# Moving the second weight slot of a split-precision decoder layer off the 128-byte grid

## The chip, the cores and the metric

The kernel runs on one core of a Trainium2 chip. Its time is device microseconds (us) of that core for one execution; lower is better. SBUF, the on-chip memory, has 128 partitions, and an address below is a byte offset inside a partition. Every tile of the kernel is placed by hand at such an offset.

## The reference

One decoder layer on 512 tokens of width 1024, in float32: a half SwiGLU feed-forward (1024 to 2 x 2816 to 1024), then a token mixer (a causal pooling branch beside an 8-head latent attention, each gated by a sigmoid), then a second half feed-forward. Each of the three is normalised and modulated by a vector `c`. Cut to what sets the work:

```python
h = modulate(rms_norm(x, norm_ffn1[l]), mod[:, 0, 0], mod[:, 0, 1])
x = x + 0.5 * mod[:, 0, 2][:, None, :] * swiglu(h, w_ffn1_in[l], w_ffn1_out[l])
h = modulate(rms_norm(x, norm_mix[l]), mod[:, 1, 0], mod[:, 1, 1])
u_pool, q_lat, kv_lat, k_rope, g_pool, g_mla = jnp.split(h @ w_in[l], split_pts, axis=-1)
...
merged = jax.nn.sigmoid(g_pool) * br_pool + jax.nn.sigmoid(g_mla) * br_mla
x = x + mod[:, 1, 2][:, None, :] * (merged @ w_out[l])
h = modulate(rms_norm(x, norm_ffn2[l]), mod[:, 2, 0], mod[:, 2, 1])
x = x + 0.5 * mod[:, 2, 2][:, None, :] * swiglu(h, w_ffn2_in[l], w_ffn2_out[l])
```

## The kernel before, in words

Each float32 product is made of three products in the type fp32r: both operands are split into a rounded half "hi" and the rest "lo", and `product` (lines 450 to 452) issues hi x hi, lo x hi and hi x lo into the same PSUM bank. The first operand is the stationary one (loaded into the array by a weight load of 128 columns), the second is the moving one (128 to 512 columns streamed past it). In the trace a matmul is written `bank<-moving,stationary`, so `bank<-h_hi,w_lo` has a tile of `w_lo` as the stationary operand.

The weights come in chunks of up to 2048 float32 values a partition (8 KB). There are two slots, and chunk n uses slot n % 2. For each chunk SyncE loads `w_raw[slot]` from HBM, ScalarE rounds it into `w_hi[slot]` (`split`, L894, and L1152, L1129, L1191 for pieces), VectorE subtracts to get `w_lo[slot]` (L1300, L1489, L1438, L1831), and TensorE then uses both, while the other slot is filled. The semaphores `raw_in`, `hi_done`, `lo_done` and `pe_used` order these steps; nothing in them depends on an address.

TensorE goes through the chunks in a fixed order. In each feed-forward there are 22 "up" chunks (48 matmuls each) and 16 "down" chunks (33 matmuls each). Three chunks have other places: the first up chunk of the first feed-forward and the second of the second one lie in `w0_raw`, `w0_hi`, `w0_lo`. In the mixer there are 24 chunks. In the feed-forwards, the pool projection, the gates, the attention projection and `w_out` the weights are the stationary operand. In three places of the mixer (the latent projection with 224 columns, the kv projection with 512 and the q projection with 384) the weights are the moving operand.

Tiles are laid out one behind the other by `place`, from offset 16512 on, which is 129 times 128. `x`, `h_hi`, `h_lo`, the six weight tiles (`w_raw`, `w_hi`, `w_lo`, two of each), `const_sb` and `ones_r` have sizes that are multiples of 128 bytes, so each of them begins at a multiple of 128. Behind them come small tiles of 32 bytes, and so the scratch tiles `scaled`, `h32`, `ssq` and `q_now` begin 64 bytes past a multiple of 128 in both kernels. A line rounds `phase_at` up to a multiple of 128 again, and the tiles of the phases (`act_hi`, `act_lo`, `sq_last`, `p_hi`, `v_hi` and the rest) begin at multiples of 128. A stationary tile of 128 float32 columns is 512 bytes of each partition, at a multiple of 512 bytes from the start of its slot.

Of the kernel before, what the change touches and what calls it, by code (L numbers as in the profile page):

```python
# [8 lines left out]
F32R = mybir.dt.float32r  # L9
AX_X = mybir.AxisListType.X  # L10

P = 128
# [17 lines left out]
SLOT = 2048  # L30
# [40 lines left out]
def program(nc, x_t, x_rows, c_rows, w_ada, w_ffn_in, w_ffn_out, w_mix, mix_consts, positions, consts, out):  # L71
    ctx = ExitStack()
    with ctx:
        cursor = [16512]

        def place(name, shape, dt=F32, at=None):

            size = 4
            for n in shape[1:]:
                size *= n  # L80
            if at is None:
                at = cursor[0]
                cursor[0] += (size + 31) // 32 * 32
            assert at + size <= 229344, (name, at + size)
            return nc.alloc_sbuf_tensor_at(name, shape, dt, offset=at)
# [8 lines left out]
        square_note = [place(f"square_note{i}", [P, D], at=cursor[0] + 4 * D * i) for i in range(TOK)]  # L94
        h_lo = place("h_lo", [P, KD, S], F32R)
        w_raw = [place(f"w_raw{i}", [P, SLOT]) for i in range(2)]
        w_hi = [place(f"w_hi{i}", [P, SLOT], F32R) for i in range(2)]
        w_lo = [place(f"w_lo{i}", [P, SLOT], F32R) for i in range(2)]
        const_sb = place("const_sb", [P, P + 72 + 3 * KD])
        ident, bias_ada, gain = const_sb[:, 0:P], const_sb[:, P:P + 72], const_sb[:, P + 72:P + 72 + 3 * KD]  # L100
        ones_r = place("ones_r", [P, P], F32R)
# [1957 lines left out]
```

## Time and profile before

| | before |
|---|---|
| median of 3 runs | 1080.08 us (1080.05 to 1080.58) |
| the profiled execution, its own time | 1080.13 us |
| span of its trace, first to last instruction | 1078.3 us |
| mean granted TensorE clock | 0.997 of full |
| TensorE matmuls | 5086, busy 1047.6 us |

The span is the part of the profiled execution that the trace shows; 1.8 us of its own time lie outside. Matmuls are pipelined: the duration of one (some 0.39 us) reaches beyond the start of the next, so the pace is read from starts, not from durations. The weight load (PEld) of a matmul runs beside the matmul before it.

### The profile page before, as it was taken

The page shows a single profiled execution, that of the slowest core. Times are in us where ns is not written, and L with a number is a line of the kernel's source. Part 1 is how long each engine was busy: PE and PEld are TensorE (multiplying, and loading weights), DVE is VectorE, ACT ScalarE, POOL GpSimd, SP SyncE. Part 2 cuts the span into 40 slices and gives each one's busy share as a digit, 9 for nine tenths or more (in the row PEclk, how much of TensorE's full clock was granted, in tenths as well). Part 3 has the DMA queues.
Part 4 walks back from the last instruction along what each step waited for, and adds up shares of the span by engine and source line. Part 5 has one row for each costly group of instructions (what it writes and reads, how often), then busy time and mean ns, then how long its engine had stood idle before and what let it go on. Part 6 is the DMA issues. An engine that isn't in the chain of part 4 may idle for free.

```text
span 1078.3 us, 13108 instructions
## 1 busy us (share of the span) xinstructions
PE 1047.6 (97%) x5086; PEld 882.5 (82%) x5086; DVE 533.2 (49%) x719; ACT 370.4 (34%) x520; POOL 71.6 (7%) x56
## 2 busy tenths in 40 slices
PE   3999999999999999998999999999999999999998
PEld 2888888888888899896888887898888888888887
DVE  5765555554663274677565455474232333322221
ACT  6643232323222143574544443333232323222211
POOL 0000000000000100851000004200000000000000
PEclk9999999999999999998999999999999999999999
DMA  9864545454763322221121122322323232222322
GB/s 353 302 242 179 202 187 197 193 186 167 248 234 123 123 82 101 71 97 60 40 78 40 77 78 79 118 79 79 117 78 117 78 115 79 92 81 85 103 88 97
DMA packets 28878, 138.62 MB, mean 129 GB/s; under 512 B 3248, under 2 KB 3504, under 8 KB 21168
## 3 DMA queue, kind: packets, MB, share of 16 engines
q1 hardware_dynamic: 28848, 138.23, 36.0%
q8 instruction: 18, 0.29, 0.1%
q14 instruction: 12, 0.10, 0.0%
HBM read 136.12 MB, written 2.10 MB: 128 GB/s over the span
## 4 chain that ended last, share of the span: by engine, by line
PE 87%; DVE 5%; POOL 3%; ACT 2%; issue 1%; DMA 1%; SPq 1%; DVEq 0%; POOLq 0%; ACTq 0%
PE bank L450 28%; PE bank L451 28%; PE bank L452 27%; PE bank L794 2%; POOL window L1957 1%; DMA ada_first<-w_ada 1%; PE bank L810 1%; DVE qk_tok L1548 1%; POOL u_pad L1963 1%; DVE w_lo L1300 1%; POOL window L1962 1%; PE bank L776 1%; ACT w_hi L894 1%; POOL h L1986 0%; DVE mvar L1654 0%
## 5 line engine op out<-in xcount | busy, mean ns | idle before, releaser
L450 PE MATMUL bank<-h_hi,w_hi 128*128 128x512 f32 (+1 forms) x976 | 373.3, 382 | 3.7 <-DVE h_lo L1495 2.8
L451 PE MATMUL bank<-h_hi,w_lo 128*128 128x512 f32 (+1 forms) x976 | 370.6, 380 | 0.0
L452 PE MATMUL bank<-h_lo,w_hi 128*128 128x512 f32 (+1 forms) x976 | 370.3, 379 | 0.0
L1300 DVE TENSOR_TENSOR w_lo<-w_raw,w_hi 128x2048 fp32r<-128x2048 f32 (+3 forms) x93 | 190.6, 2049 | 155.3 <-ACT w_hi L894 155.3
L450 PEld LDWEIGHTS bank<-h_hi,w_hi 128*128 128x128 f32 x976 | 184.1, 189 | 41.0 <-DVE h_lo L1495 3.2
L452 PEld LDWEIGHTS bank<-h_lo,w_hi 128*128 128x128 f32 x976 | 184.0, 189 | 34.9
L451 PEld LDWEIGHTS bank<-h_hi,w_lo 128*128 128x128 f32 x976 | 184.1, 189 | 33.6
L894 ACT ACTIVATE w_hi<-w_raw 128x2048 fp32r<-128x2048 f32 (+3 forms) x93 | 159.0, 1710 | 119.4 <-PE bank L452 75.9
L450 PE MATMUL bank<-act_hi,w_hi 128*128 128x512 f32 (+1 forms) x374 | 141.1, 377 | 0.0
L452 PE MATMUL bank<-act_lo,w_hi 128*128 128x512 f32 (+1 forms) x374 | 140.8, 377 | 0.0
L451 PE MATMUL bank<-act_hi,w_lo 128*128 128x512 f32 (+1 forms) x374 | 140.8, 376 | 0.0
L1178 ACT ACTIVATE scaled<-bank 128x512 f32<-128x512 f32 x44 | 26.3, 597 | 275.2 <-PE bank L452 275.2
L1818 DVE TENSOR_TENSOR scaled<-scaled,bank 128x512 f32<-128x512 f32 x44 | 30.2, 687 | 165.8 <-ACT scaled L1178 165.8
L451 PEld LDWEIGHTS bank<-act_hi,w_lo 128*128 128x128 f32 x374 | 70.4, 188 | 12.9
L452 PEld LDWEIGHTS bank<-act_lo,w_hi 128*128 128x128 f32 x374 | 70.4, 188 | 12.9
L450 PEld LDWEIGHTS bank<-act_hi,w_hi 128*128 128x128 f32 x374 | 70.4, 188 | 12.8
L1305 DVE CUSTOM_DVE_ANT_0 ada_raw<-ada_raw,c_wide,const_sb 128x1024 f32<-128x1024 f32 x56 | 69.8, 1280 | 4.4 <-DMA ada_raw<-w_ada 4.4
L1822 DVE TENSOR_TENSOR act_lo<-scaled,act_hi 128x512 fp32r<-128x512 f32 (+1 forms) x44 | 30.5, 693 | 35.6 <-ACT act_hi L1182 35.6
L1886 DVE SCALAR_TENSOR_TENSOR x<-bank,out_gate,x 128x512 f32<-128x512 f32 (+1 forms) x15 | 11.3, 751 | 61.2 <-PE bank L452 61.2
L1182 ACT ACTIVATE act_hi<-scaled 128x512 f32 (+1 forms) x44 | 27.8, 632 | 38.9 <-DVE scaled L1818 38.9
L903 ACT ACTIVATE scaled<-x 128x512 f32<-128x512 f32 (+1 forms) x13 | 8.2, 629 | 58.3 <-DVE x L1886 42.9
L450 PE MATMUL bank<-w_hi,h_hi 128*128 128x224 f32 x96 | 26.7, 278 | 0.7 <-DVE h_lo L1375 0.7
(191 smaller groups left out, 915.5 us busy)
## 6 DMA issues: line engine op xcount, KB each, us to landing
w_raw<-w_ffn_in SPq DMA_DIRECT2D x41, 1024.0 KB, 4.8
ada_raw<-w_ada SPq DMA_DIRECT2D x56, 512.0 KB, 5.4
w_raw<-w_ffn_out SPq DMA_DIRECT2D x32, 704.0 KB, 4.0
w_raw<-w_mix SPq DMA_DIRECT2D x19, 1024.0 KB, 4.8
ada_first<-w_ada SPq DMA_DIRECT2D x16, 512.0 KB, 12.7
w_raw<-w_ffn_in SPq DMA_DIRECT2D x6, 512.0 KB, 12.7
w_raw<-w_mix SPq DMA_DIRECT2D x3, 896.0 KB, 4.6
x_tok<-x_rows SPq DMA_DIRECT2D x4, 512.0 KB, 6.7
```

The source lines that it names most:

```text
L450: nc.tensor.matmul(dst, a_hi, b_hi, start=start, stop=False)
L451: nc.tensor.matmul(dst, a_lo, b_hi, start=False, stop=False)
L452: return nc.tensor.matmul(dst, a_hi, b_lo, start=False, stop=stop)
L794: nc.tensor.matmul(bank[qt][:, 0:(qt + 1) * P], q_now[0:HEAD, toks(qt)], k_t[0:HEAD, bass.ds(h, 1), 0:(qt + 1) * P], start=True, stop=False)
L894: nc.scalar.activation(w_hi[slot][:, 0:size], w_raw[slot][:, 0:size], ACT.Copy).then_inc(hi_done, 1)
L1178: nc.scalar.activation(silu_g, bank[banks[0]][:, :], ACT.Silu).then_inc(silu_done, 1)
L1182: nc.scalar.activation(act_hi[f][:, bass.ds(j, 1), :], prod, ACT.Copy).then_inc(act_hi_done, 1)
L1300: nc.vector.tensor_tensor(w_lo[slot][:, 0:size], w_raw[slot][:, 0:size], w_hi[slot][:, 0:size].bitcast(F32), ALU.subtract).then_inc(lo_don ...
L1305: nc.vector.tensor_tensor_reduce(out=raw, in0=raw, in1=c_wide[:, :], scale=1.0, scalar=bias_ada[:, col:col + 1], op0=ALU.mult, op1=ALU.add ...
L1818: nc.vector.tensor_tensor(prod, silu_g, bank[banks[1]][:, :], ALU.mult).then_inc(gu_evac, 1)
L1822: nc.vector.tensor_tensor(act_lo[f][:, bass.ds(j, 1), :], prod.unsqueeze(1), act_hi[f][:, bass.ds(j, 1), :].bitcast(F32), ALU.subtract)\
L1886: nc.vector.scalar_tensor_tensor(out=xm, in0=bank[4 + s // 2][:, :].unsqueeze(1), scalar=out_gate[:, bass.ds(m, 1)], in1=xm, op0=ALU.mult, ...
```

## The change

It gives the second slot of `w_hi` and of `w_lo` an offset of its own. `w_hi[0]` stays where it was, and `w_hi[1]` begins 64 bytes later than before. 128 bytes are reserved for each pair, so that `w_lo[0]` moves by 128 bytes (still at a multiple of 128), `w_lo[1]` by 192 (64 past a multiple of 128), and everything behind by 256. `w_raw` stays. No instruction, wait or transfer is added, removed or moved, and each keeps its shape.

```diff
         w_raw = [place(f"w_raw{i}", [P, SLOT]) for i in range(2)]
-        w_hi = [place(f"w_hi{i}", [P, SLOT], F32R) for i in range(2)]
-        w_lo = [place(f"w_lo{i}", [P, SLOT], F32R) for i in range(2)]
+        slot = 4 * SLOT
+        w_hi = [place(f"w_hi{i}", [P, SLOT], F32R, at=cursor[0] + (slot + 64) * i) for i in range(2)]
+        cursor[0] += 2 * slot + 128
+        w_lo = [place(f"w_lo{i}", [P, SLOT], F32R, at=cursor[0] + (slot + 64) * i) for i in range(2)]
+        cursor[0] += 2 * slot + 128
```

## Rows read from the trace of the kernel before

**Rows 1.** The page: span, and busy time, share and instructions of each engine.

```profile
span 1078.3 us, 13108 instructions
PE 1047.6 (97%) x5086; PEld 882.5 (82%) x5086; DVE 533.2 (49%) x719; ACT 370.4 (34%) x520; POOL 71.6 (7%) x56
```

**Rows 2.** The longest waits of TensorE: engine, line, releaser, us in total, times, longest.

```profile
PE bank L505 <- DVE x_tok L1505: 15.3, 1, 15.3
PE bank L776 <- DVE qk_tok L1548: 4.7, 1, 4.7
PE bank L450 <- DVE h_lo L1495: 2.8, 1, 2.8
```

**Rows 3.** Timeline of PE, two up chunks: start us, duration us, what.

```profile
770.10 0.39 PE L450 MATMUL bank<-h_hi,w_hi 128*128 128x512 f32 x1
...
780.75 0.39 PE L452 MATMUL bank<-h_lo,w_hi 128*128 128x512 f32 x1
780.98 0.39 PE L450 MATMUL bank<-h_hi,w_hi 128*128 128x512 f32 x1
...
791.63 0.39 PE L452 MATMUL bank<-h_lo,w_hi 128*128 128x512 f32 x1
```

**Rows 4.** Timeline of PE, matmuls of 256 columns in the last chunk of `w_out`.

```profile
699.74 0.28 PE L452 MATMUL bank<-h_lo,w_hi 128*128 128x256 f32 x1
...
705.98 0.28 PE L450 MATMUL bank<-h_hi,w_hi 128*128 128x256 f32 x1
```

**Rows 5.** Timeline of PEld, weight loads for matmuls of one column.

```profile
714.68 0.30 PEld L470 LDWEIGHTS bank<-ones_r,ssq 128*128 128x128 f32 x2
714.91 0.53 PEld L472 LDWEIGHTS bank<-ones_r,sq_last 128*128 128x128 f32 x4
715.36 0.30 PEld L470 LDWEIGHTS bank<-ones_r,ssq 128*128 128x128 f32 x2
715.58 0.53 PEld L472 LDWEIGHTS bank<-ones_r,sq_last 128*128 128x128 f32 x4
716.03 0.19 PEld L450 LDWEIGHTS bank<-h_hi,w_hi 128*128 128x128 f32 x1
```

**Rows 6.** Timeline of PE, latent projection, weights moving, 224 columns.

```profile
391.93 0.28 PE L451 MATMUL bank<-w_hi,h_lo 128*128 128x224 f32 x1
...
393.05 0.27 PE L452 MATMUL bank<-w_lo,h_hi 128*128 128x224 f32 x1
```

**Rows 7.** ScalarE groups by shape: line, op, tiles, count, busy us, mean ns, idle before.

```profile
L1178 ACT ACTIVATE scaled<-bank 128x512 f32<-128x512 f32 x44 | 26.3, 597 | 275.2 <-PE bank L452 275.2
L1182 ACT ACTIVATE act_hi<-scaled 128x512 f32 x34 | 21.5, 632 | 30.0 <-DVE scaled L1818 30.0
L972 ACT ACTIVATE p_hi<-bank 128x512 fp32r<-128x512 f32 x16 | 8.7, 599 | 0.0
L1152 ACT ACTIVATE w_hi<-w_raw 128x512 fp32r<-128x512 f32 x3 | 1.8, 626 | 0.0
```

**Rows 8.** VectorE groups by shape.

```profile
L1822 DVE TENSOR_TENSOR act_lo<-scaled,act_hi 128x512 fp32r<-128x512 f32 x26 | 18.0, 692 | 18.9 <-ACT act_hi L1182 18.9
L1489 DVE TENSOR_TENSOR w_lo<-w_raw,w_hi 128x512 fp32r<-128x512 f32 x3 | 2.0, 687 | 0.0
```

**Rows 9.** Timelines of ACT and DVE, the split for the chunk that follows.

```profile
772.36 1.90 ACT L894 ACTIVATE w_hi<-w_raw 128x2048 fp32r<-128x2048 f32 x1
774.30 2.29 DVE L1300 TENSOR_TENSOR w_lo<-w_raw,w_hi 128x2048 fp32r<-128x2048 f32 x1 [0.99 <-ACT w_hi L894]
```

**Rows 10.** Line L1300: who waited for it, us in total and times.

```profile
PEld bank L450: 0.5, 1
```

## The prediction

> **What bounds the kernel now.** I read the page first: TensorE is busy for 1047.6 of 1078.3 us, VectorE for 49% and ScalarE for 34% [rows 1]. The waits of TensorE came next. The long ones are three, 15.3 us at the start, 4.7 us before the turned heads and 2.8 us in the first chunk, and none is for a split of weights [rows 2]. So the time is the number of matmuls times the pace at which they start, and that is what an address could change.
>
> The pace is read from starts in the timeline. In the second feed-forward the chunk that starts at 770.10 us has its weights in slot 1 and the next in slot 0. In both, 47 intervals between the first and the last start take 10.65 us, so 226.6 ns each [rows 3]: the slots are alike today, as both are on the grid. For 256 columns, 52 intervals take 6.24 us, 120.0 ns each [rows 4]. The 256 columns between the two cost 106.6 ns, which is 2.4 GHz, so 512 columns are 213.3 ns and each pair of weight load and matmul costs **13.3 ns more than its columns**. That fixed part is where a clash of the two readers, or its absence, would be. When the columns are few the weight load sets the pace: the 12 loads from 714.68 to 716.03 us take 1.35 us, 112.5 ns each [rows 5].
>
> **The change, part by part.** It moves `w_hi[1]` and `w_lo[1]` to 64 bytes past a multiple of 128, `w_lo[0]` by 128 bytes and all behind by 256.
>
> How much work reads slot 1, counted from the code: as the stationary operand with 512 columns, 528 matmuls in the up part of the first feed-forward and 231 in its down part, 480 and 264 in the second, and in the mixer 48 (pool input), 12 (groups), 48 (pool projection), 192 (four gates), 48 (attention projection) and 48 (`w_out`), together 1899. With 256 columns it is 66 in the last down part and 96 in the last chunk of `w_out`, together 162. So 2061 matmuls have a shifted stationary operand. As the moving operand: 96 of 224 columns, 48 of 512 and 36 of 384, together 180.
>
> *Loads of a shifted stationary tile.* The trace has them already. `ssq` begins 64 bytes past a multiple of 128 and `sq_last` at a multiple. The loads run in turns: two of `ssq` take 0.23 us (714.68 to 714.91) and 0.22 us (715.36 to 715.58), so 0.1125 us each, and four of `sq_last` take 0.45 us both times, 0.1125 us each [rows 5]. A load from the 64-byte start is as fast, in the stretch in which the load alone sets the pace. Cost: 2061 x 0 = 0. What these rows don't show is such a load beside 512 moving columns; that is the unknown of this case. I bound it from below by the whole fixed part given back, -13.3 ns, and from above by the same once more, +13.3 ns, and take 0, since the nearest rows are alike to the 0.01 us that the view gives.
>
> *A shifted moving operand.* No row shows one of the fp32r products. In the latent projection the moving slices begin 896 bytes apart, so by turns at an even and an odd multiple of 128; ten intervals take 1.12 us, 112 ns, with no step between slices [rows 6]. That is for shifts of 128 and over, which is also what happens to `w_lo[0]` and to all that moves by 256: cost 0. For 64 bytes I bound it by the same 13.3 ns either way: 180 x 13.3 ns = 2.4 us, and take 0.
>
> *The splits.* ScalarE writes a tile on the shifted grid (`scaled`) in 597 ns and one at a multiple of 128 (`p_hi`) in 599 ns, and reads the shifted one in 632 ns against 626 ns for `w_raw` [rows 7]. VectorE takes 692 ns with a shifted input and 687 ns without [rows 8]. So 1% of 2.29 us at most, and it is hidden: the split for the chunk at 780.98 us is done at 774.30 + 2.29 = 776.59 us [rows 3, 9], 4.4 us early. The only place where TensorE waited for a split of whole chunks is 0.5 us, once [rows 10]; 1% of a split there is 0.03 us. Were the cover gone everywhere, 1% of some 46 splits of slot 1 at 2.3 us would be 1 us. DMAs write `w_raw`, which stays.
>
> **Sum:** 0 + 0 + 0.03 us on the profiled execution's own 1080.13 us (its span of 1078.3 us and 1.8 us outside), which is 0.05 us above the median of the runs. The forecast is 1080.1 us.
>
> A rule of the notes bears on the fixed part. The Trainium skill, "SBUF — State Buffer", section "Specifications (TRN2)", says that SBUF is read by lines of 16 bytes, and 64 bytes are a whole number of these. By that rule nothing changes, and the trace agrees as far as it goes, in the equal 112.5 ns of [rows 5]. The Trainium skill, "TensorE: Matmul & The Clock Gate", section "Part 2: What happens when you issue a matmul", gives TensorE two independent read ports, one for weight loads and one for the moving operand. It speaks against any gain here: by it the sum stays 0, where a clash would leave up to 27 us to win. No run here has shown yet which of the two the 13.3 ns are.
>
> **The rivals.**
>
> *A. The two readers of TensorE clash, and the shift ends it: faster.* For it: the 13.3 ns are there in every pair, of 512 as of 256 columns [rows 3, 4], and today the stationary tile and the moving tile both begin on the grid, in every fp32r product, so the trace can't tell a clash from a fixed cost. Against it: the pace doesn't differ between tiles whose distance is another multiple of 128 [rows 3, 6]. Price: 1899 x 13.3 ns = 25.3 us; for the 162 of 256 columns the load sets a floor of 112.5 ns, so 162 x 7.5 ns = 1.2 us; together 26.5 us, 1053.6 us. If half the clash is ended, 1066.9 us. It decides from 2.16 us / 2061 = 1.05 ns a matmul on.
>
> *B. A stationary tile that straddles the grid costs more: slower.* Its 512 bytes lie in 4 pieces of 128 bytes today and would touch 5. For it: the load beside a running matmul is not in the rows. Against it: [rows 5]. If the fixed part grows with the pieces, 13.3 / 4 = 3.3 ns x 2061 = 6.9 us, 1087.0 us. If only the load's own time grows by a quarter, 112.5 to 140.6 ns, it stays hidden under 226.6 ns, and shows in the 162 matmuls of 256 columns, 120 to 141 ns, 3.3 us: 1083.4 us. If each fixed part doubles, 2061 x 13.3 ns = 27.4 us, 1107.5 us. It decides from the same 1.05 ns a matmul.
>
> *C. Only the moving operand minds:* 180 x 13.3 ns = 2.4 us, 1082.5 us; smaller costs would not be seen.
>
> **How the numbers follow.** Two runs of this kernel can tell about 0.2% from nothing, 2.2 us. No change that can be measured: 0.62, since each operand that the shift touches has a row or two that show no cost, except the pair of readers together. A: 0.14, half of it at 1066.9 us or nearer to the forecast. B: 0.20, of which 0.13 at 1083 to 1087 us and 0.07 beyond. C: 0.04. The predicted time is that of the likeliest, 1080.1 us, whose own range is 1079.3 to 1081.2 us. To leave out no more than 2 in 10 the range takes in the two smaller forms of B, C, and the near part of A up to a quarter of the clash, 26.5 / 4 = 6.6 us below: 1073.5 to 1087.5 us. Faster 0.14, same 0.62, slower 0.24.
>
> **What would show each step right or wrong.** In the timeline of the changed kernel, the 47 intervals of the chunk at 770 us (slot 1) against those of the next (slot 0): 10.65 us both by the forecast; 10.0 us in slot 1 by A; 10.8 us by the first form of B. In the last chunk of `w_out`, 120 ns a matmul of 256 columns by the forecast, 141 ns by the second form of B. In the latent projection the slices of `w_hi[1]` at 112 ns, as those of slot 0, or more by C. The groups of L894 and L1300 keep their means within 1%. What would make the forecast wrong is a pace that depends on both readers at once, in the one combination that the trace before doesn't hold.

## The result, and the profile after

The changed kernel takes 1096.28 us (median of 4 runs, 1095.71 to 1097.75) against 1080.33 us for the kernel before (median of 4). The ratio is 1.0147 with a 95% interval of 1.0135 to 1.016. The change makes the kernel 1.5% slower, where no measurable change was forecast.

The page of the changed kernel: span, and busy time, share and instructions of each engine.

```profile
span 1094.8 us, 13108 instructions
PE 1063.2 (97%) x5086; PEld 883.3 (81%) x5086; DVE 533.2 (49%) x719; ACT 370.6 (34%) x520; POOL 72.2 (7%) x56
```

Against [rows 1] the span has grown by 16.5 us and the busy time of TensorE by 15.6 us, with the same 5086 matmuls. VectorE and ScalarE are as busy as before. The waits of TensorE (engine, line, releaser, us in total, times, longest) are also what they were in [rows 2], to 0.7 us each:

```profile
PE bank L508 <- DVE x_tok L1508: 16.0, 1, 16.0
PE bank L779 <- DVE qk_tok L1551: 4.2, 1, 4.2
PE bank L453 <- DVE h_lo L1498: 3.1, 1, 3.1
```

So the pace itself has changed. The timeline of PE in the changed kernel, the same two up chunks as in [rows 3], first slot 1 and then slot 0 (all lines are three further on, 453 for 450):

```profile
757.78 0.39 PE L453 MATMUL bank<-h_hi,w_hi 128*128 128x512 f32 x1
...
768.67 0.40 PE L455 MATMUL bank<-h_lo,w_hi 128*128 128x512 f32 x1
768.91 0.39 PE L453 MATMUL bank<-h_hi,w_hi 128*128 128x512 f32 x1
...
770.29 0.40 PE L453 MATMUL bank<-h_hi,w_hi 128*128 128x512 f32 x1
770.52 0.40 PE L454 MATMUL bank<-h_hi,w_lo 128*128 128x512 f32 x1
770.76 0.39 PE L455 MATMUL bank<-h_lo,w_hi 128*128 128x512 f32 x1
770.99 0.40 PE L453 MATMUL bank<-h_hi,w_hi 128*128 128x512 f32 x1
...
779.77 0.39 PE L455 MATMUL bank<-h_lo,w_hi 128*128 128x512 f32 x1
```

The 47 intervals take 10.89 us in slot 1 (231.7 ns each) and 10.86 us in slot 0 (231.1 ns), where both took 10.65 us (226.6 ns). **Slot 0 is as slow as slot 1**, although no tile of it is off the 128-byte grid. In slot 0 the intervals repeat in threes: 0.23, 0.24, 0.23 us in the rows, and 233, 234, 227 ns in the starts to the nanosecond. Two of three cost 6 to 7 ns more: the one that begins at the matmul with a tile of `w_lo`, and the one before it, beside which that tile is loaded.

5.1 ns for the 1899 matmuls of 512 columns that read slot 1, and 4.5 ns for some 1887 that read slot 0, are 9.7 + 8.5 = 18.2 us. The span grew by 16.5 us. The starts in the traces show where the rest is. The 3833 intervals that begin at a matmul of 512 columns with a stationary weight tile sum to 879.7 us before and 895.8 us after, 16.1 us more. Those under 300 ns went from a mean of 227.0 to 231.7 ns, which is some 18 us, and the waits in the longer ones shrank by 1.8 us. TensorE also started 0.7 us later. And the matmuls of 256 columns have become faster. The last chunk of `w_out`, slot 1, the same stretch as in [rows 4], timeline of PE:

```profile
709.07 0.28 PE L455 MATMUL bank<-h_lo,w_hi 128*128 128x256 f32 x1
...
714.97 0.28 PE L453 MATMUL bank<-h_hi,w_hi 128*128 128x256 f32 x1
```

The 52 intervals take 5.90 us, 113.5 ns each, where [rows 4] have 120.0 ns. Not all are so fast: the 420 intervals of 256 columns with a weight tile, waits among them, sum to 0.5 us less than before.

### The profile page after: what moved, and what is told of

The parts are those of the page before. It is cut to its first block, busy times and chain, and to the rows that moved or that the text cites. A ratio compares the mean times of both kernels' runs of the same rounds, so it can differ in the third digit from the quotient of the medians.

```text
span 1094.8 us, 13108 instructions
## 1 busy us (share of the span) xinstructions
PE 1063.2 (97%) x5086; PEld 883.3 (81%) x5086; DVE 533.2 (49%) x719; ACT 370.6 (34%) x520; POOL 72.2 (7%) x56
## 4 chain that ended last, share of the span: by engine, by line
PE 87%; DVE 5%; POOL 3%; ACT 2%; DMA 1%; issue 1%; SPq 1%; DVEq 0%; POOLq 0%; ACTq 0%
PE bank L454 28%; PE bank L453 28%; PE bank L455 27%; PE bank L797 2%; DMA ada_first<-w_ada 1%; POOL window L1960 1%; PE bank L813 1%; POOL u_pad L1966 1%; DVE qk_tok L1551 1%; DVE w_lo L1303 1%; POOL window L1965 1%; PE bank L779 1%; ACT w_hi L897 1%; POOL h L1989 0%; DVE mvar L1657 0%
## 5 line engine op out<-in xcount | busy, mean ns | idle before, releaser
L454 PE MATMUL bank<-h_hi,w_lo 128*128 128x512 f32 (+1 forms) x976 | 376.2, 385 | 0.0
L454 PE MATMUL bank<-act_hi,w_lo 128*128 128x512 f32 (+1 forms) x374 | 143.2, 383 | 0.0
```

Source lines behind the costliest of these rows:

```text
L454: nc.tensor.matmul(dst, a_lo, b_hi, start=False, stop=False)
```

## The experiments

Slot 0 speaks against the rival that was priced for a slower kernel (a tile that straddles the grid). What differs in slot 0 is that `w_lo[0]` has moved by 128 bytes, while `w_hi[0]`, `h_hi` and `h_lo` stayed. Three theories follow. **R**: the pace depends on the distance, modulo some period, between the stationary tile that is being loaded and the moving tile that is being streamed. **D**: it depends on the distance between one stationary tile and the next (`w_hi` to `w_lo`). **G**: a tile off the grid costs, wherever the others are. The first six runs are the whole layer with other offsets; their edits stand in place of the lines of the change. `shift_hi` and `shift_lo` are bytes by which the two tiles of `w_hi` and of `w_lo` begin later than in the kernel before. The ratio of each run is to the kernel before on the same chip, with its 95% interval behind it.

**e1: the 128 bytes alone.**

```diff
+        shift_hi, shift_lo = (0, 0), (128, 128)
+        w_hi = [place(f"w_hi{i}", [P, SLOT], F32R, at=cursor[0] + 4 * SLOT * i + shift_hi[i]) for i in range(2)]
+        w_lo = [place(f"w_lo{i}", [P, SLOT], F32R, at=cursor[0] + 4 * SLOT * (2 + i) + shift_lo[i]) for i in range(2)]
+        cursor[0] += 16 * SLOT + 256
```

> Both tiles of w_lo move by 128 bytes, w_hi stays, nothing is 64 bytes past the grid; all behind moves by 256. Theory R (the pace depends on the distance between the places from which the two readers of TensorE read, taken modulo 256 or more, so the 128 bytes between w_hi and w_lo cost as much as the 64): slower as the changed kernel, about 231 ns for each matmul of 512 columns, 1094 to 1097 us. Theory G (a stationary tile that begins off the 128-byte grid costs more, and the slowness of slot 0 in the changed kernel is an after-effect of slot 1): 226.7 ns, 1080 us.

1095.27 us, ratio 1.0136 (1.0119 to 1.0152). With every weight tile on the 128-byte grid the kernel is nearly as slow as with the change. Both slots now have the pattern of threes. The timeline of PE in e1, a chunk of slot 0:

```profile
770.01 0.40 PE L452 MATMUL bank<-h_hi,w_hi 128*128 128x512 f32 x1
...
780.87 0.39 PE L454 MATMUL bank<-h_lo,w_hi 128*128 128x512 f32 x1
```

10.86 us for 47 intervals, as slot 0 of the changed kernel. Theory G is out as the explanation of slot 0.

**e2: the 64 bytes alone.** The edit, against that of e1:

```diff
-        shift_hi, shift_lo = (0, 0), (128, 128)
+        shift_hi, shift_lo = (0, 64), (256, 320)
-        cursor[0] += 16 * SLOT + 256
+        cursor[0] += 16 * SLOT + 512
```

> w_hi[1] is 64 bytes past the grid as in the change; w_lo[0] moves by 256 and w_lo[1] by 320 instead of 128 and 192, so that w_hi and w_lo of slot 0 are again a multiple of 256 bytes apart. Theory R with a period of 256: slot 0 is back at 226.7 ns; slot 1 is at its own pace, which depends on 64 bytes between the stationary and the moving tile; if that alone costs the 5.1 ns of slot 1 in the changed kernel, 1089 to 1091 us. Theory D (only the distance between w_hi and w_lo counts): both slots at 226.7 ns, 1080 us. Theory G: slot 1 at 231 to 232 ns, slot 0 unchanged, 1089 to 1091 us.

1092.47 us, ratio 1.0112 (1.0096 to 1.0129), 1.5 us above the top of what R gave. The timeline of PE in e2, slot 1 and then slot 0:

```profile
754.98 0.40 PE L452 MATMUL bank<-h_hi,w_hi 128*128 128x512 f32 x1
...
765.95 0.39 PE L454 MATMUL bank<-h_lo,w_hi 128*128 128x512 f32 x1
766.17 0.39 PE L452 MATMUL bank<-h_hi,w_hi 128*128 128x512 f32 x1
...
776.86 0.39 PE L454 MATMUL bank<-h_lo,w_hi 128*128 128x512 f32 x1
```

Slot 0, with its tiles a multiple of 256 bytes from each other, is back: 10.69 us, 227.4 ns, and 226.7 ns once the first few intervals are over. Slot 1 takes 10.97 us, 233.4 ns, more than the 231.7 ns of the change. There `w_hi[1]` is 64 and `w_lo[1]` 192 bytes off modulo 256; here both are 64 off. I had taken the wrong pace for this slot: 1899 x 6.7 ns = 12.7 us against 12.0 us measured. Theory D is out as the cause of this loss, since `w_hi` and `w_lo` of slot 1 are a multiple of 256 apart.

**e4: both slots by 64 bytes** (`shift_hi, shift_lo = (64, 64), (64, 64)`, `cursor[0] += 16 * SLOT + 256`).

> All four tiles of w_hi and w_lo begin 64 bytes past the grid, their distances as in the kernel before; all behind moves by 256. Theory D (only the distance between w_hi and w_lo counts): 1080 us. Theory G (off the grid costs): twice the matmuls of the change that are off it, so 1096 to 1110 us. Theory R (distance between stationary and moving tile): not 226.7 ns in most matmuls; the sign is open.

1103.12 us, ratio 1.0214 (1.0197 to 1.0231). The timeline of PE in e4, slot 1:

```profile
761.44 0.39 PE L452 MATMUL bank<-h_hi,w_hi 128*128 128x512 f32 x1
...
772.40 0.40 PE L454 MATMUL bank<-h_lo,w_hi 128*128 128x512 f32 x1
```

10.96 us, 233.2 ns. This fits G as well as R, so the next ones separate them.

**e5: everything by 64 bytes**, the moving tiles too.

```diff
-        cursor = [16512]
+        cursor = [16512 + 64]
...
-        cursor[0] = (cursor[0] + 2048 + 127) // 128 * 128
+        cursor[0] = (cursor[0] + 2048 + 127) // 128 * 128 + 64
```

> Every tile of the kernel, moving and stationary, lies 64 bytes further on, so that all that was at a multiple of 128 is 64 bytes off it. Theory R: all distances are as before, 226.7 ns and 1080.3 us. Theory G (a tile off the 128-byte grid costs, and e4 was slow because its four tiles were off it): at least the 1103 us of e4.

1080.14 us, ratio 1.0001 (0.9991 to 1.0011). The timeline of PE in e5, slot 1:

```profile
748.16 0.39 PE L450 MATMUL bank<-h_hi,w_hi 128*128 128x512 f32 x1
...
758.82 0.39 PE L452 MATMUL bank<-h_lo,w_hi 128*128 128x512 f32 x1
```

10.66 us. The four weight tiles lie 64 bytes off the grid as in e4, and the pace is that of the kernel before. It is the distance to the moving tile that counts, not the address. Theory G is out.

**e3: only what lies behind, by 256 bytes** (`shift_hi, shift_lo = (0, 0), (0, 0)`, `cursor[0] += 16 * SLOT + 256`).

> Only what lies behind w_lo moves, by 256 bytes, as in the change; w_hi and w_lo stay. Theory R (distance between stationary and moving tile modulo 256): act_hi and act_lo, attn_hi and the others move by a whole period, so 226.7 ns everywhere and 1080.3 us. Rival (the move of the tiles behind is part of the slowness): above 1082.5 us.

1080.23 us, ratio 1.0001 (0.9992 to 1.0011). A distance changed by 256 bytes costs nothing, and this part of the change is innocent.

**e6: both slots by 192 bytes** (`shift_hi, shift_lo = (192, 192), (192, 192)`, `cursor[0] += 16 * SLOT + 256`).

> The four tiles of w_hi and w_lo begin 192 bytes later, all moving tiles stay at their places modulo 256. Theory R with the paces of the scan (228.9 ns at a distance of 192, 233.3 at 64): 2.2 ns more for each of some 3786 matmuls of 512 columns, 8.4 us, less 0.7 us for those of 256 columns, so 1086.5 to 1089 us. Rival (only whether the tiles are at a multiple of 128 matters, 64 or 192 alike): 1103 us as e4.

1087.61 us, ratio 1.0069 (1.0052 to 1.0086), as worked out from the scan below. Two offsets off the grid differ by 15.5 us, 192 bytes against 64.

**m1, a scan of distances.** Its core, in a loop over the layouts, each run once; `a` and `b` are the shifts in bytes, and two matmuls of 64 columns stand before each block of 36:

```python
if kind == "single":
    st, at, mv = hi, (a + step * (i % 16)) // 4, 0
elif kind == "moved":
    st, at, mv = hi, (a + step * (i % 16)) // 4, b // 4
...
last = nc.tensor.matmul(bank[c % 7][:, 0:n], st[:, at:at + P], mov[:, mv:mv + n],
                        start=i == 0, stop=i == COUNT - 1)
```

> This kernel leaves the whole layer out: it only measures the pace of fp32r matmuls, 36 in a row for each layout, weights and activations replaced by slices of one weight matrix. Moving operand of 512 columns at a multiple of 2048 bytes, stationary tiles 512 bytes apart, their first at a shift of 0, 16, 32, 48, 64, 80, 96, 112, 128, 160, 192, 224, 256, 320, 384 or 448 bytes; then the pattern of the kernel (hi, lo, hi) with two shifts; one stationary tile loaded again and again; 256 columns; and the moving operand shifted in place of the stationary. Theory R: shift 0 gives 226.7 ns, others between 216 and 240 ns, by the shift modulo 256 or 512, and a shift of the moving operand acts as one of the stationary. Theory G: 226.7 ns at 0, 128, 256 and 384, more at all others. Theory D: one pace for all shifts while hi and lo shift together, another for pairs with a distance of 64 or 128.

The timeline of PE in m1 shows each block as one row, and then the first of the two small matmuls behind it. Shifts of the stationary tile: 0, 64, 192 and 256 bytes.

```profile
41.48 8.42 PE L64 MATMUL bank<-mov,hi 128*128 128x512 f32 x36
49.74 0.19 PE L53 MATMUL bank<-mov,hi 128*128 128x64 f32 x1
...
75.75 8.64 PE L64 MATMUL bank<-mov,hi 128*128 128x512 f32 x36
84.22 0.19 PE L53 MATMUL bank<-mov,hi 128*128 128x64 f32 x1
...
127.41 8.50 PE L64 MATMUL bank<-mov,hi 128*128 128x512 f32 x36
135.75 0.19 PE L53 MATMUL bank<-mov,hi 128*128 128x64 f32 x1
...
144.51 8.42 PE L64 MATMUL bank<-mov,hi 128*128 128x512 f32 x36
152.76 0.19 PE L53 MATMUL bank<-mov,hi 128*128 128x64 f32 x1
```

From the start of a block to the matmul behind it: 8.26 us at 0, 8.47 at 64, 8.34 at 192, 8.25 at 256. The mean of the last 18 intervals of each block, from the starts in the trace, 512 columns in fp32r:

| shift of the stationary tile, bytes | ns for each matmul |
|---|---|
| 0, 256 | 226.7 |
| 192, 448 | 228.9 |
| 80 | 232.0 |
| 128, 384 | 232.5, 232.8 |
| 16, 32, 48, 64, 112, 160, 224, 320 | 233.3 |
| 96 | 234.1 |
| moving tile shifted by 16, 32, 64, 96, 128 | 232.0, 233.3, 228.9, 233.4, 233.3 |
| pattern of `product`, shifts of hi and lo 0 and 128 | 231.4 |
| 64 and 192 | 231.9 |
| 64 and 64, 32 and 32 | 233.3 |
| 128 and 128 | 232.5 |
| 0 and 64 | 231.1 |
| 0 and 32 | 233.3 |
| 0 and 256, 0 and 0 | 226.7 |

The pace repeats after 256 bytes in all four pairs tried, to 0.3 ns. A moving tile 64 bytes further on acts as a stationary one 64 bytes back, that is 192. The two slots of the changed kernel are in the table: 0 and 128 give 231.4 ns (231.1 measured there), 64 and 192 give 231.9 (231.7). That is theory R in outline, with a period of 256 bytes.

Three rows go beyond it. First, the mixed patterns with hi at 0 are slower than their parts. With hi at 0 and lo at 128, only one of three intervals has a loaded tile at a distance other than 0 from the streamed one, and a mean of a third of 232.5 and two thirds of 226.7 ns would be 228.6 ns; 231.4 ns were measured. With lo at 32 all three intervals are slow (239, 229, 232 ns). So a tile at another distance slows its neighbours too, and R doesn't say how. Second, a moving tile shifted by 16 gives 232.0 ns, where R asks for the pace of a stationary tile at 240, which m2 has at 228.2 ns. The other mirror pairs agree within 0.8 ns. Third, a single stationary tile loaded again and again gives 226.7 ns at 0 and 233.3 at 64, as do tiles 512 bytes apart. Both are a multiple of 256 from the tile before, so this shows only that the loss needs no change of stationary tile; in the mixed patterns the distance from one stationary tile to the next may still play a part.

**m2, shared shifts, finer steps, bfloat16, fewer columns.** The same loop with other layouts.

> Leaves the layer out, as m1. Stationary and moving tile shifted together by 32, 64, 128, 192: theory R 226.7 ns each, theory G more at 32, 64 and 192. The stationary tile shifted by 4, 8, 12, 20, 144, 176, 188, 196, 208, 240, 248, 252 bytes: theory R gives a pace for each; whether one lies below 226.7 ns is open. bfloat16 tiles at 0, 32, 64, 128, 192: if the 13.3 ns are stalls by the reads of a weight load (32 reads of 16 bytes, one cycle each), half as many bytes cost some 6.7 ns, so 220 ns; if they are a fixed cost of a change of weights, 226.7 ns. Fewer columns (480 to 320) at distance 0: columns / 2.4 plus 13.3 ns by both.

With both tiles shifted by 32, 64, 128 or 192 bytes together the pace is 226.7 ns each time. Of twelve finer shifts of the stationary tile none lies below 226.7 ns: 228.2 ns at 240 is the nearest, 230.0 at 12, 232.6 at 4, 233.3 at 248 and 252. Four bytes are enough to lose the good case. With fewer columns at distance 0 the expectation of 13.3 ns over the columns held at 384 and 320 (173.3 and 146.7 ns) and missed at 480 and 448 (216.7 and 202.7 ns, 16.7 and 16.0 ns over). In bfloat16 the distance does nothing. The timeline of PE in m2, shift 0 and shift 64:

```profile
184.14 7.72 PE L64 MATMUL bank<-mb,hb 128*128 128x512 bf16 x35
191.51 0.38 PE L57 MATMUL bank<-mov,hi 128*128 128x64 f32 x1
...
199.77 7.95 PE L64 MATMUL bank<-mb,hb 128*128 128x512 bf16 x35
207.36 0.38 PE L57 MATMUL bank<-mov,hi 128*128 128x64 f32 x1
```

The mean is 215.8 ns at all five shifts, without the gap where a record is missing (some blocks are told as x35). So the 13.3 ns over the columns belong to fp32r: in bfloat16 only 2.5 ns are left. I had expected 220 or 226.7 ns, and neither came. The Trainium skill, "TensorE: Matmul & The Clock Gate", section "Wait — 56ns, not 53.3ns?", gives 215.7 ns for 512 columns back to back; the trace agrees in bfloat16 and with a weight load before each matmul, and not in fp32r.

**m3, fewer weight columns and fewer moving columns.** As m2, with `st[:, at:at + b]` and b columns loaded.

> Leaves the layer out, as m1. Distance between stationary and moving tile 0 or 64 bytes, 512 moving columns, and weight loads of 128, 96, 64 and 32 columns: if the 13.3 ns at distance 0 are stalls of the moving stream by the reads of the weight load, they fall with the columns loaded (128: 226.7 ns, 64: about 220, 32: about 217 at distance 0, and 233, 223, 218 at 64); if they are a fixed cost of a change of weights in fp32r, 226.7 and 233.3 ns at every number. Then 128 columns loaded and 496, 480, 448, 416, 384, 256 moving, at distances 0, 64 and 192: by m2 the distance costs nothing at 384 (173.3 ns) and little at 448, so the cost of the distance should appear only towards 512 columns.

| loaded columns | distance 0 | distance 64 |
|---|---|---|
| 128 | 226.7 | 233.3 |
| 96 | 230.0 | 228.2 |
| 64 | 229.9 | 232.5 |
| 32 | 231.8 | 231.6 |

The timeline of PE in m3, 128 and then 32 loaded columns, both at distance 0, 36 matmuls each:

```profile
56.34 8.42 PE L61 MATMUL bank<-mov,hi 128*128 128x512 f32 x36
...
107.22 8.51 PE L61 MATMUL bank<-mov,hi 128*32 128x512 f32 x36
```

The expectation missed: a quarter of the weights costs 5.1 ns more, not 10 ns less. So the excess isn't a stall for each piece of weights read. With 128 columns loaded, at distances 0, 64 and 192, the pace is 223.6, 226.7, 226.7 ns for 496 moving columns; 216.7, 216.1, 218.3 for 480; 202.7, 202.2, 200.0 for 448; 188.4, 186.7, 188.1 for 416; 173.3, 176.7, 173.3 for 384; 120.0, 117.8, 117.8 for 256. At 384 columns and a distance of 64, m2 had 173.3 ns, steady through its block, and m3 has 176.7 ns, steady too. The same layout can thus settle 3.4 ns apart, and single differences of that size in the scans prove little; the mirror pair of 16 and 240 is one. At 512 columns each block at a multiple of 256 settled at 226.7 ns (but for the first of m2 and of m3, which settle only in their last 12 intervals), and each block with all tiles at a distance of 64 at 233.3 ns, in every scan that has them. Over the scans 0 is the best distance at 512 columns, by 1.5 to 7.4 ns, and the worst at 256. The layer goes the same way at both widths, at 256 columns even further (113.5 ns in the stretch above).

## Why the prediction was wrong, point by point

**What bounds the kernel** was right: TensorE's pace, with 13.3 ns over the columns at 512 and at 256, read from [rows 3, 4]. It isn't a fixed part at every width: m3 has 16.9 ns at 496 columns. By the prediction 1.05 ns a matmul decide, and the change moved the pace by 4.5 to 5.1 ns. The sign that it named for a wrong forecast, 10.65 us for 47 intervals in both slots, came out as 10.89 and 10.86 us.

**The step that failed** is the cost of a load of a shifted stationary tile, taken as "2061 x 0 = 0" from [rows 5]. Those loads stand beside matmuls of one moving column. They show that the load alone doesn't mind its address, which may well be so, and they can't show what happens when a load runs beside 512 streamed columns. The text named this gap as the unknown and then took 0 "since the nearest rows are alike". The nearest rows were not near: they held one of the two readers still. By the code, moreover, `ones_r`, the moving tile there, lies at 0 modulo 256, `ssq` at 64 and `sq_last` at 128, so neither load stood for distance 0. The runs showed +6.7 ns at a distance of 64 bytes, and for the mixed pairs of the change +4.5 to 5.1 ns in the layer and +4.7 and 5.2 ns in the scan, within the bound of +13.3 ns that was written down, and outside the range that was made of it.

**A second step failed with it**: "for shifts of 128 and over ... cost 0", which was said of `w_lo[0]`. It rested on [rows 6], where the moving slices alternate between even and odd multiples of 128. At 224 columns the pace is 112 ns, that of the loads alone in [rows 5], and so these rows can't show what the stream would do. Slot 0 gave half of the loss (1887 x 4.5 ns = 8.5 us), and e1 shows it alone: 14.7 us for 128 bytes on all of `w_lo`.

**Rival A** noted that in all products both tiles begin at the same place of the grid, "so the trace can't tell a clash from a fixed cost". That was the right observation, with the sign turned round: the equal place is the good case, and every one of the 23 other distances tried at 512 columns is worse. Its argument against itself, that the pace doesn't differ "between tiles whose distance is another multiple of 128", had no row at 512 columns: all tiles of [rows 3] lie at 128 modulo 256, so every distance there is a multiple of 256. **Rival B** forecast slower with forms of 1083.4, 1087.0 and 1107.5 us. Its mechanism, the pieces of the grid that a tile touches, was wrong: e5 has the same off-grid tiles as e4 at 1080.14 us, and e1 has none and is slow. That its first form gave 10.8 us for slot 1, near the 10.89 us measured, was luck. **Rival C** held in part: the kv projection with moving weights at 512 columns has 47 intervals in the trace whose mean rose from 227.2 to 230.3 ns, which is 0.15 us.

**The splits** cost nothing, as forecast. Groups of DVE and ACT by shape in the changed kernel, against [rows 7, 8]:

```profile
L1825 DVE TENSOR_TENSOR act_lo<-scaled,act_hi 128x512 fp32r<-128x512 f32 x26 | 18.0, 693 | 18.9 <-ACT act_hi L1185 18.9
L1155 ACT ACTIVATE w_hi<-w_raw 128x512 fp32r<-128x512 f32 x3 | 1.8, 627 | 0.0
```

**The rule of two independent read ports** was weighed against a gain. By it no loss was to be expected either, and the runs show one. The Trainium skill, "TensorE: Matmul & The Clock Gate", section "Part 2: What happens when you issue a matmul", says that loading the next weights doesn't take read bandwidth from the running matmul. For fp32r the measurement decides: the pace goes from 226.7 to 233.3 ns with nothing changed but where the loaded tile lies. In bfloat16, 215.8 ns at five distances, the trace agrees with the rule. The prediction also took a shift by whole 16 bytes to be free, and in fp32r it isn't: m1 has 233.3 ns at 16, 32, 48 and 64 bytes.

**What stays open.** Shown is that at 512 columns a distance of 0 modulo 256 bytes is the fast case, wherever the tiles lie, and that other distances cost 1.5 to 7.4 ns. Which of them costs how much is known from single blocks only, and how one such tile slows its neighbours in a mixed pattern isn't known. The reason isn't shown either: two streams that share something with a period of 256 bytes would be a guess, m3 contradicts its simple form (a stall for each piece of weights read), and no run looks inside. Nor is it shown why other counts of moving columns don't favour distance 0. No layout tried is faster than the kernel before, so there is no better version to offer for this change; the kernel before has the best of the distances tried, in all its fp32r products of 512 columns.

## What to carry to other kernels

In fp32r, keep every stationary tile and every moving tile of 512 columns a multiple of 256 bytes apart; it was worth up to 2.1% of this kernel, which TensorE bounds, and the tiles moved by 256 bytes in e3 cost no time. For matmuls of 256 columns the scans don't bear the rule out. When a cost is bounded by "the nearest row", ask which of the two partners of the interaction that row holds still: a row in which the load sets the pace says nothing about the stream, and one with a single moving column says nothing about 512. When a change moves several things, compare first a part that it was not meant to touch, here slot 0.

## What the runs showed of the hardware that was not expected

- The pace of back-to-back fp32r matmuls of 512 columns, each with its own weight load, is 226.7 ns at a distance of 0 modulo 256 bytes and 228.2 to 234.1 ns at the others tried; a distance of 4 bytes already gives 232.6 ns.
- Moving stationary and moving tiles together costs nothing: all tiles 64 bytes further on leave 1080.14 us, and common shifts of 32, 64, 128 and 192 bytes leave 226.7 ns.
- One tile of three away from distance 0 slows its neighbours: hi at 0 and lo at 32 bytes take 233.3 ns, as much as both at 32.
- The same stream in bfloat16 takes 215.8 ns at each of the five distances tried.
- Loading 32 weight columns in place of 128 makes the stream slower at distance 0, 231.8 against 226.7 ns.
- At 256 moving columns the order turns: 120.0 ns at distance 0, 117.8 at 64 and at 192.
